# TensorE's loop over the eight experts written out as straight code

## The chip, the cores and the metric

The kernel runs on one NeuronCore of a Trainium2 chip. The metric is device time in microseconds (us) of one execution; lower is better. The kernel before was timed in three runs: median 2112.82 us, lowest 2110.67, highest 2112.97. A separate execution was taken with the hardware profiler; its numbers are those of the profile.

Five engines work side by side, each with its own list of instructions: TensorE (PE in the profile; its weight loads are PEld), VectorE (DVE), ScalarE (ACT), GpSimd (POOL) and SyncE (SP), which here only starts transfers. They meet through semaphores.

## The reference

A sequence of 256 tokens with 1024 features passes through two mixer layers, the second of which ends in a mixture of eight experts, and then through two layers of another block. What the change touches is the mixture of experts:

```python
def moe_swiglu(xn, router_w, w_gate_up, w_down):
    b_, s_, d_ = xn.shape
    xf = xn.reshape(-1, d_)
    logits = (xf @ router_w).astype(jnp.float32)
    top_v, top_i = lax.top_k(logits, TOP_K)
    top_w = jax.nn.softmax(top_v, axis=-1)
    combine = jnp.sum(jax.nn.one_hot(top_i, N_EXPERTS, dtype=jnp.float32) * top_w[..., None],
                      axis=1).astype(xn.dtype)
    out = jnp.zeros_like(xf)
    for e in range(N_EXPERTS):
        out = out + combine[:, e:e + 1] * swiglu(xf, w_gate_up[e], w_down[e])
    return out.reshape(b_, s_, d_)
```

with 8 experts, 2 chosen for each token, and a hidden width of 3584. The weights of one expert are 1024 x 7168 and 3584 x 1024 numbers in float32: 44.04 MB.

## The kernel before

The program is one long list for each engine, in stages: mixer, feed-forward network, mixer, router, experts, and two layers of the second block. Nearly all of it is straight code: the Python that writes it runs over constants. The expert stage is an exception. There each engine has a hardware loop: a body that is in the program once, a register `e` that counts, and a branch from the end of the body back to its start.

For each expert, up to 96 tokens are gathered (`xg`, four groups of 32 columns are used at a time, so one matmul covers a quarter of the array). `token_experts` holds TensorE's part. Its inner function `expert(e, follows)` does, in this order:

- `up("EG", 0, e)` and `up("EU", 0, e)`: gate and up projection of the first 2048 hidden units, four weight tiles of 2 MB each (L1371, 128x512 results);
- the first of the four tiles of `up("EG", 1, e)`, then `first_half_turned`: the hidden values are transposed (L1089), and the numbers of the rows that the next expert needs are computed (L1426);
- the rest of `up("EG", 1, e)` and `up("EU", 1, e)`: the other 1536 hidden units, tiles of 1.5 MB (L1371, 128x384);
- `down(0, e, o)`, the transposes of the second half and, where another expert follows, of the rows gathered for it (L1089), then `down(1..6, e, o)`: the down projection in seven tiles of 2 MB (L1407).

In all an expert has 16 tiles of up weights and 7 of down weights. The function is written into the loop for experts 0 to 6 (`follows` true) and once more behind it for expert 7 (`follows` false). In the profile a float32 matmul of the source appears as two matmuls and two weight loads: 768 of L1371 and 672 of L1407 for each expert.

Waits in the body name a semaphore and a value. In the loop the value is computed from the register `e` (`at(e, ...)`, `tiles.before(name, e)`, `freed(job, i)`); in `begin` a wait whose value is known and not above zero is left out.

The weights come through a ring of five slots of 2 MB. SP's list has its own loop (L955): for every tile it waits until TensorE has freed the slot (`tile_free`, L916) and starts two transfers (L919). So a tile is asked for when the one five places earlier has been used. ScalarE's and VectorE's loops (L2321, L3165) evict results from the banks and form the hidden values; GpSimd's (L1935) fetches the rows of the next expert.

Behind the expert stage the second block begins with the matmuls of L1016 at 1611 us. `more` is the register that TensorE loads before the loop and tests after it, for a further pass that is only run when an expert has more than 96 tokens; the profile shows no such pass.

Of the kernel before, what the change touches and what calls it, by code (L numbers as in the profile page):

```python
# [33 lines left out]
D_FF, EXPERTS, D_EXP = 2816, 8, 3584  # L34
# [365 lines left out]
def kernel_program(nc, t):  # L400
# [30 lines left out]
    with ctx:  # L431
# [354 lines left out]
        def drained(job, i=None):  # L786
            r, s = (banks_f, f_bank_free) if job in banks_f.place else (banks, bank_free)
            return s[r.slot(job)], r.freed(job, i) + 1
# [21 lines left out]
        def at(i, per, n):  # L810
            return n if i is None else i * per + n
# [168 lines left out]
        def _(pe):  # L980
            def begin(job, i=None):

                r, s = (banks_f, f_bank_free) if job in banks_f.place else (banks, bank_free)
                known = i is None or isinstance(i, int)
                if not known or r.freed(job, i) > 0:
                    pe.wait_ge(s[r.slot(job)], r.freed(job, i))
                return bank[r.slot(job)]

            def end(job, i=None):

                if job in closes:
                    return tile_end(closes[job])
                if closing_half(job, i) is not None:
                    return raw_end(closing_half(job, i))
                r, s = (banks_f, f_bank_full) if job in banks_f.place else (banks, bank_full)
                return s[r.slot(job)], 1
# [88 lines left out]
            def turn(job, src, i=None, order=ident):  # L1085

                o = begin(job, i)
                for k, v in enumerate(src):
                    mm = pe.transpose(o[:, k * P:(k + 1) * P], v, order)  # L1089
                mm.then_inc(*end(job, i))  # L1090
# [266 lines left out]
            def token_experts(meanwhile):  # L1357
# [19 lines left out]
                def up(kind, half, e, between=None):  # L1377
                    o = [begin((kind, "m", half, i), e) for i in range(TRIPLE)]
                    for k in range(4):
                        up_tile(kind, half, k, e, o)  # L1380
                        if k == 0 and between is not None:
                            between()

                def turn_gated(half, e):
                    for i in range(TRIPLE):
                        pe.wait_ge(*drained(("EU", "m", half, i), e))
                        turn(("ET", "m", half, i), [gated[half][:, i, k * P:(k + 1) * P] for k in range(UNITS_OF[half] // P)], e)

                def turn_sel(job, groups, e):
                    o = begin(job, e)  # L1390
                    for k, (i, b) in enumerate((i, b) for i in groups for b in range(TB)):
                        for z in range(QUADS):
                            mm = pe.matmul(o[GROUP * z:GROUP * (z + 1), k * P:(k + 1) * P],
                                           sel[:, b, GROUP * i:GROUP * (i + 1)], ident, start=True, stop=True)
                    mm.then_inc(*end(job, e))

                def down(k, e, o):
                    name = ("ED", "m", k)
                    weights(name, e)
                    w = tile_view(name, 4, D)  # L1400
                    for c in range(4):
                        n = 4 * k + c
                        half = n >= HALF // P
                        z, jb = divmod(n - half * HALF // P, UNITS_OF[half] // P)
                        for i in range(TRIPLE):
                            for q in range(QUADS):
                                mm = pe.matmul(o[i // 2][GROUP * q:GROUP * (q + 1), Q_D * (i % 2):Q_D * (i % 2 + 1)],  # L1407
                                               hidT_m[half][:, i, jb, GROUP * z:GROUP * (z + 1)],
                                               w[:, c, Q_D * q:Q_D * (q + 1)], start=n == 0 and i != 1,
                                               stop=n == EX_CH - 1 and i != 0)  # L1410
                            if n == EX_CH - 1 and i == 1:
                                mm.then_inc(*end(("Y", "m", 0)))
                    mm.then_inc(*tile_end(name))

                def expert(e, follows):
                    pe.wait_ge(*drained(("GX", "m", 1), e))
                    up("EG", 0, e)
                    up("EU", 0, e)

                    def first_half_turned():  # L1420
                        turn_gated(0, e)
                        if follows:
                            pe.wait_ge(sel_ready, e + 2)
                            o = begin(("IX", "m"), e)
                            for b in range(TB):
                                mm = pe.matmul(o[:, 0:8], sel_r[:, b, :], token_ids[:, b, :], start=b == 0, stop=b == TB - 1)  # L1426
                            mm.then_inc(*end(("IX", "m")))
                        else:
                            turn_sel(("IX", "m"), (0, 1), e)

                    up("EG", 1, e, first_half_turned)
                    up("EU", 1, e)
                    o = [begin(("Y", "m", n), e) for n in range(2)]
                    for i in range(TRIPLE):
                        pe.wait_ge(*drained(("ET", "m", 0, i), e))
                    down(0, e, o)
                    turn_gated(1, e)
                    if follows:
                        pe.wait_ge(rows_fetched, at(e, 16, 16))
                        for hf in range(2):  # L1440
                            turn(("GX", "m", hf), [x_rows[:, c * P:(c + 1) * P] for c in range(4 * hf, 4 * hf + 4)], e + 1)
                    else:
                        turn_sel(("SX",), (2,), None)
                    for k in range(1, EX_PAIRS):
                        if 4 * (k + 1) > HALF // P >= 4 * k:
                            for i in range(TRIPLE):
                                pe.wait_ge(*drained(("ET", "m", 1, i), e))
                        down(k, e, o)
# [2 lines left out]
                pe.wait_ge(flag_ready, 1)  # L1451
                more = pe.value_load(flag_word)
                meanwhile()
                with pe.Fori(0, EXPERTS - 1) as e:
                    expert(e, True)
                expert(EXPERTS - 1, False)
                return more

            def experts(r, sel_sem):
# [144 lines left out]
            def last_keys():  # L1604
                memory_keys(0, 1, False).then_inc(*end(("EK", 0)))
                memory_keys(1, 1, False).then_inc(*end(("EK", 1)))

            more = token_experts(last_keys)
            pe.br_cond(more > 0, "tensor_overflow", "tensor_second_block")
            home = nc.cur_bb  # L1610
# [2046 lines left out]
```

## Time and profile before

| | |
|---|---|
| median of three runs | 2112.82 us (2110.67 to 2112.97) |
| span of the profiled execution | 2110.0 us |
| TensorE busy | 2067.8 us, 98% of the span |
| VectorE, ScalarE, GpSimd busy | 857.3, 699.9, 46.7 us |
| moved by DMA | 570.95 MB, mean 271 GB/s |
| expert stage, from the first L1371 matmul to the first L1016 matmul behind it | 668.1 to 1611.1 us |

The profiled execution has a span of 2110.0 us; the times of the runs lie 0.7 to 3.0 us above it, the median 2.8 us. Busy time of an engine says how much of the span it was working, not how much could be saved: what counts is the engine that sets the end, and the stretches in which that engine stands still or works slower than it could. The profile also gives the granted clock of TensorE (1.00 is the full 2.4 GHz, 0.50 is 1.2 GHz) for any stretch, and the share in which the core's 16 DMA engines were busy (a little above 1 where packets overlap).

### The profile page before, as it was taken

To read this page: it belongs to the slowest core of one execution; us is meant where nothing else is said; L and a number is where in the kernel's file an instruction comes from. 1 tells how busy PE (TensorE), PEld (TensorE's weight loads), DVE (VectorE), ACT (ScalarE), POOL (GpSimd) and SP (SyncE) were. 2 spreads that over 40 slices of the span, in tenths; PEclk is the share of its full clock that TensorE was granted. 3 is DMA by queue.
4 is the path that set the end of the run, shared out by engine and by line. 5 is a ranking of instruction groups with operands and counts; after the bars stand their busy time and mean duration, and the time that the engine had idled before them with its cause. 6 is when DMAs were issued, how large, how long until landed. Compare 5 with 4: busy or idle time off the path is not lost.

```text
span 2110.0 us, 40789 instructions
## 1 busy us (share of the span) xinstructions
PE 2067.8 (98%) x17747; PEld 1371.6 (65%) x17747; DVE 857.3 (41%) x1203; ACT 699.9 (33%) x950; POOL 46.7 (2%) x69
## 2 busy tenths in 40 slices
PE   9999999999999989989999999999999999999998
PEld 6888888888887343525344353524447888888887
DVE  6876655468764000000000000000024878677775
ACT  5565544455653000001000000001004455555552
POOL 5000000000000000000000000000000000000000
PEclk9999999999999999999999999999999999999999
DMA  9654655554557998999989898999998644455442
GB/s 300 163 183 154 228 190 180 177 197 155 200 180 277 382 413 332 412 355 391 403 346 412 333 413 334 411 358 388 418 394 324 206 146 159 147 195 185 140 160 81
DMA packets 174391, 570.95 MB, mean 271 GB/s; under 512 B 13209, under 2 KB 26273, under 8 KB 157570
## 3 DMA queue, kind: packets, MB, share of 16 engines
q1 hardware_dynamic: 165376, 546.74, 69.9%
q0 software_dynamic: 5280, 17.16, 2.5%
q10 hardware_dynamic: 3554, 4.33, 0.6%
q8 instruction: 151, 2.47, 0.5%
q14 instruction: 30, 0.25, 0.0%
HBM read 562.80 MB, written 5.39 MB: 269 GB/s over the span
## 4 chain that ended last, share of the span: by engine, by line
PE 97%; issue 2%; DMA 1%; DVE 0%; ACT 0%; DVEq 0%; POOL 0%; SPq 0%; ACTq 0%; POOLq 0%
PE bank L1016 39%; PE bank L1371 28%; PE bank L1407 13%; PE bank L1071 5%; PE bank L1089 3%; PE bank L1078 3%; PE bank L1022 1%; DMA ring<-moe_w_down 1%; PE bank L1115 0%; PE bank L1637 0%; PE bank L1644 0%; PE bank L1645 0%; PE bank L1665 0%; PE bank L1651 0%; PE bank L1643 0%
## 5 line engine op out<-in xcount | busy, mean ns | idle before, releaser
L1371 PE MATMUL bank<-ring,xT 128*32 128x512 f32 (+1 forms) x6144 | 591.9, 547 | 31.0 <-issue 31.0
L1016 PE MATMUL bank<-halves_r,x_both 128*128 128x512 f32 x2624 | 607.8, 390 | 0.0
L1016 PEld LDWEIGHTS bank<-halves_r,x_both 128*128 128x128 f32 x2624 | 489.9, 188 | 101.8 <-issue 1.5
L1371 PEld LDWEIGHTS bank<-ring,xT 128*32 128x32 f32 x6144 | 195.7, 111 | 419.6 <-issue 419.2
L2607 DVE TENSOR_TENSOR halves_r<-ring,halves_r 128x2048 fp32r<-128x2048 f32 x170 | 383.8, 2288 | 124.0 <-ACT halves_r L2025 122.9
L2025 ACT ACTIVATE halves_r<-ring 128x2048 fp32r<-128x2048 f32 x172 | 324.9, 1913 | 157.6 <-DMA ring<-w_in 69.7
L3136 DVE TENSOR_TENSOR arena<-arena,bank 128x512 f32<-128x512 f32 (+1 forms) x48 | 29.8, 621 | 773.8 <-PE bank L1371 772.4
L1407 PE MATMUL bank<-ring,arena 128*32 128x256 f32 x5376 | 293.4, 379 | 0.5 <-DMA ring<-moe_w_down 0.5
L1407 PEld LDWEIGHTS bank<-ring,arena 128*32 128x32 f32 x5376 | 175.7, 110 | 115.9 <-issue 5.2
L2288 ACT ACTIVATE arena<-bank 128x512 f32<-128x512 f32 (+1 forms) x48 | 22.6, 545 | 360.3 <-PE bank L1089 360.3
L2212 ACT ACTIVATE arena<-bank 128x512 f32<-128x512 f32 (+1 forms) x58 | 32.1, 554 | 285.0 <-PE bank L1371 252.4
L1071 PE MATMUL bank<-x_both,halves_r 128*128 128x512 f32 x448 | 107.3, 391 | 0.3 <-DVE x_both L3421 0.3
L1071 PEld LDWEIGHTS bank<-x_both,halves_r 128*128 128x128 f32 x448 | 82.4, 188 | 18.4 <-issue 1.6
L1016 PE MATMUL bank<-halves_r,yT_high 128*128 128x512 f32 x256 | 80.7, 392 | 0.0
L2301 ACT ACTIVATE arena<-bank 128x512 f32<-128x512 f32 (+1 forms) x14 | 6.1, 487 | 210.8 <-PE bank L1407 210.8
L1089 PE MATMUL bank<-consts,arena 128*128 128x128 f32 x508 | 65.4, 274 | 0.0
L1089 PEld LDWEIGHTS bank<-consts,arena 128*128 128x128 f32 x508 | 57.1, 141 | 11.1 <-issue 8.3
L1078 PEld LDWEIGHTS bank<-x_both,halves_r 128*128 128x128 f32 x448 | 57.4, 191 | 2.2
L1078 PE MATMUL bank<-x_both,halves_r 128*128 128x256 f32 x448 | 58.1, 283 | 0.0
L1016 PE MATMUL bank<-halves_r,hidT_high 128*128 128x512 f32 x176 | 55.0, 391 | 0.0
L1016 PEld LDWEIGHTS bank<-halves_r,yT_high 128*128 128x128 f32 x256 | 47.9, 188 | 9.8
L2003 ACT ACTIVATE arena<-bank 128x512 f32<-128x512 f32 x54 | 30.9, 597 | 68.0 <-PE bank L1016 54.1
(412 smaller groups left out, 1533.2 us busy)
## 6 DMA issues: line engine op xcount, KB each, us to landing
ring<-moe_w_gate_up SPq DMA_DIRECT2D x128, 1024.0 KB, 13.1
ring<-moe_w_down SPq DMA_DIRECT2D x112, 1024.0 KB, 11.4
ring<-w_in SPq DMA_DIRECT2D x99, 1024.0 KB, 5.2
ring<-moe_w_gate_up SPq DMA_DIRECT2D x128, 768.0 KB, 8.5
ring<-w_out SPq DMA_DIRECT2D x24, 1024.0 KB, 5.0
ring<-ffn_w_gate_up SPq DMA_DIRECT2D x20, 1024.0 KB, 5.3
ring<-ffn_w_down SPq DMA_DIRECT2D x11, 1024.0 KB, 4.9
ring<-w_in SPq DMA_DIRECT2D x18, 512.0 KB, 6.4
```

The lines of the kernel that those rows point to most:

```text
L1016: return pe.matmul(o[:, a:a + n], x[:, c, b * P:(b + 1) * P], w[:, k, col:col + n], **flags)
L1071: mm = pe.matmul(shaped(o[:, :], 2, SEQ), w[:, k, j * P:(j + 1) * P], x_pair[:, :, c, :], start=c == 0, stop=False)
L1078: mm = pe.matmul(o[:, 0:SEQ], w[:, k, j * P:(j + 1) * P], xT_high[:, c, :], start=False, stop=c == KC - 1)
L1089: mm = pe.transpose(o[:, k * P:(k + 1) * P], v, order)
L1371: mm = pe.matmul(o[i][GROUP * z:GROUP * (z + 1), 0:u], xg[:, c, GROUP * i:GROUP * (i + 1)], w[:, q, u * z:u * (z + 1)], start=c == 0, stop ...
L1407: mm = pe.matmul(o[i // 2][GROUP * q:GROUP * (q + 1), Q_D * (i % 2):Q_D * (i % 2 + 1)], hidT_m[half][:, i, jb, GROUP * z:GROUP * (z + 1)], ...
L2003: act.activation(dst, src, func, scale=scale).then_inc(*fr(job))
L2025: act.activation(top_view(half), raw_view(half), ACT.Copy).then_inc(top_in, 1)
L2212: act.activation(dst, out_of(job)[:, 0:n], ACT.Silu).then_inc(*fr(job))
L2288: act.activation(flat(hidT_m[half][:, i, :, :]), out_of(("ET", "m", half, i))[:, 0:UNITS_OF[half]], ACT.Copy).then_inc(*fr(("ET", "m", hal ...
L2607: dve.tensor_tensor(raw_view(half, halves_r), raw_view(half), top_view(half).bitcast(F32), ALU.subtract).then_inc(raw_low_in, 1)
L3136: dve.tensor_tensor(v, v, out_of(("EU", "m", half, i))[:, 0:UNITS_OF[half]], ALU.mult).then_inc(*fr(("EU", "m", half, i)))
```

## The change

In `token_experts`, the loop of TensorE is taken out. A Python loop calls `expert` eight times with a constant `e`, so the body is in TensorE's list eight times, with constant values in its waits. No other engine's list is changed; the loops of SP, ScalarE, VectorE and GpSimd stay.

```diff
--- before.py
+++ after.py
@@ -1451,9 +1451,8 @@
                 pe.wait_ge(flag_ready, 1)
                 more = pe.value_load(flag_word)
                 meanwhile()
-                with pe.Fori(0, EXPERTS - 1) as e:
-                    expert(e, True)
-                expert(EXPERTS - 1, False)
+                for e in range(EXPERTS):
+                    expert(e, e < EXPERTS - 1)
                 return more
```

## Rows read from the trace of the kernel before

**Rows 1.** The page: span; busy time and share; tenths in 40 slices; chain by engine.
```profile
span 2110.0 us, 40789 instructions
PE 2067.8 (98%) x17747; PEld 1371.6 (65%) x17747; DVE 857.3 (41%) x1203; ACT 699.9 (33%) x950; POOL 46.7 (2%) x69
...
PEclk9999999999999999999999999999999999999999
...
PE 97%; issue 2%; DMA 1%; DVE 0%; ACT 0%; DVEq 0%; POOL 0%; SPq 0%; ACTq 0%; POOLq 0%
```

**Rows 2.** TensorE's waits, 640 to 1612 us: releaser, total us, times, longest.
```profile
PE bank L1371 <- issue: 31.0, 6, 5.3
PE bank L1407 <- DMA ring<-moe_w_down: 0.5, 1, 0.5
```

**Rows 3.** TensorE's timeline, expert 0: start, length, instructions [idle before, releaser].
```profile
668.13 45.28 PE L1371 MATMUL bank<-ring,xT 128*32 128x512 f32 x432
...
714.92 27.30 PE L1371 MATMUL bank<-ring,xT 128*32 128x384 f32 x336
...
749.33 31.29 PE L1407 MATMUL bank<-ring,arena 128*32 128x256 f32 x576
```

**Rows 4.** The same timeline: the first block of experts 1 to 7, with expert 1's second.
```profile
785.96 47.25 PE L1371 MATMUL bank<-ring,xT 128*32 128x512 f32 x432 [5.34 <-issue]
...
834.72 27.30 PE L1371 MATMUL bank<-ring,xT 128*32 128x384 f32 x336
...
905.70 47.11 PE L1371 MATMUL bank<-ring,xT 128*32 128x512 f32 x432 [5.28 <-issue]
...
1025.11 47.15 PE L1371 MATMUL bank<-ring,xT 128*32 128x512 f32 x432 [5.08 <-issue]
...
1144.53 47.16 PE L1371 MATMUL bank<-ring,xT 128*32 128x512 f32 x432 [5.07 <-issue]
...
1264.02 47.16 PE L1371 MATMUL bank<-ring,xT 128*32 128x512 f32 x432 [5.11 <-issue]
...
1383.52 47.14 PE L1371 MATMUL bank<-ring,xT 128*32 128x512 f32 x432 [5.13 <-issue]
...
1497.68 45.25 PE L1371 MATMUL bank<-ring,xT 128*32 128x512 f32 x432
```

**Rows 5.** Stretches: us, busy (count) by engine, granted clock, DMA share, GB/s.
```profile
16.00:640.00 624.00, 624.00 (x2982) 516.38 (x2981) 416.34 (x480) 340.55 (x411) 23.58 (x34) 1.00 0.58 187
780.00:786.00 6.00, 0.66 (x16) 0.18 (x11) 0.00 (x0) 2.15 (x3) 0.00 (x0) 0.76 1.01 415
786.00:790.00 4.00, 4.00 (x20) 0.95 (x24) 0.00 (x0) 0.00 (x0) 0.00 (x0) 0.50 1.02 416
790.00:795.00 5.00, 5.00 (x52) 1.47 (x48) 0.00 (x0) 0.00 (x0) 0.00 (x0) 1.00 1.01 404
1612.00:2100.00 488.00, 487.07 (x2697) 419.26 (x2696) 363.77 (x559) 259.37 (x355) 3.72 (x7) 1.00 0.49 162
```

**Rows 6.** The same view, for the transfers: the last two columns, DMA share and GB/s.
```profile
749.00:780.00 31.00, 31.00 (x572) 18.65 (x574) 0.65 (x3) 1.15 (x3) 0.00 (x0) 1.00 1.03 413
786.00:833.00 47.00, 47.00 (x432) 13.45 (x432) 2.07 (x3) 1.79 (x3) 0.00 (x0) 0.96 0.87 332
1430.60:1466.60 36.00, 36.00 (x470) 17.35 (x467) 1.82 (x4) 4.49 (x10) 0.94 (x1) 1.00 1.00 396
1497.70:1518.00 20.30, 20.30 (x196) 6.23 (x192) 0.00 (x0) 1.59 (x4) 0.00 (x0) 1.00 1.02 421
1518.00:1543.00 25.00, 25.00 (x249) 7.80 (x238) 2.06 (x3) 0.87 (x2) 0.00 (x0) 1.00 0.98 384
```

**Rows 7.** DMA queues from 785.9 to 905.6: packets, MB, share of 16 engines.
```profile
q1 hardware_dynamic: 8416, 44.04, 93.1%
q0 software_dynamic: 144, 0.52, 1.2%
q10 hardware_dynamic: 446, 0.39, 1.0%
q8 instruction: 13, 0.21, 0.8%
```

**Rows 8.** The instruction queue, 668.1 to 780.6 and then 1497.7 to 1611.
```profile
q8 instruction: 11, 0.18, 0.6%
...
q8 instruction: 12, 0.20, 0.7%
```

**Rows 9.** SP's loads: expert 1's first tile, its last up tile, expert 7's first tile.
```profile
L919 SPq DMA_DIRECT2D ring<-moe_w_gate_up x2: 356/360/363, 760.2 to 760.7; - x2
DMA to landing us min/median/max: 13.4/14.9/16.5
...
L919 SPq DMA_DIRECT2D ring<-moe_w_gate_up x2: 333/400/467, 842.9 to 843.4; - x2
DMA to landing us min/median/max: 9.4/11.0/12.7
...
L919 SPq DMA_DIRECT2D ring<-moe_w_gate_up x2: 345/345/345, 1477.4 to 1477.9; - x2
DMA to landing us min/median/max: 13.4/14.8/16.1
```

**Rows 10.** SP's waits, 1497 to 1611 us: us, times, longest.
```profile
SPq L916 <- PE bank L1371: 56.7, 14, 9.2
SPq L916 <- PE bank L1407: 13.8, 3, 5.7
```

**Rows 11.** The fetch of the next expert's rows: start of the instruction, time to landing.
```profile
L1940 POOL DMA_INDIRECT arena<-normalised_rows,arena x1: 965/965/965, 836.1 to 836.1; - x1
...
DMA to landing us min/median/max: 9.4/9.4/9.4
```

**Rows 12.** ScalarE's timeline about the end of expert 1.
```profile
900.06 0.87 ACT L2301 ACTIVATE arena<-bank 128x512 f32<-128x512 f32 x2 [30.11 <-PE bank L1407]
...
926.70 0.60 ACT L2212 ACTIVATE arena<-bank 128x512 f32<-128x512 f32 x1 [22.20 <-PE bank L1371]
```

## The prediction

> **What bounds the kernel now.** The page comes first: TensorE is busy for 98% of the span and makes up 97% of the chain that ended last, so the end is set by TensorE, and only its own idle or slow time can be saved. The chain has 2% of "issue" beside it: time in which TensorE waited for nothing that the profile shows [rows 1]. The view of TensorE's waits says where that is: six waits before L1371, 31.0 us together, and in the whole expert stage only one other, of 0.5 us [rows 2]. The timeline then places the six. They stand before the first matmul of experts 1 to 6, each 5.07 to 5.34 us long. There is none before expert 0, where the loop is entered, and none before expert 7, where it is left [rows 3, 4]. The loop over experts 0 to 6 has exactly six branches back. The same body, the same waits on semaphores and the same tiles come at the step from expert 6 to 7, without a gap; only the branch back is missing there. So I read the idle as the price of that branch: TensorE's sequencer has no instructions until the start of the body has been brought in again.
>
> **A second cost at the same place.** The first block of an expert (432 matmuls) takes 45.28 us in expert 0 and 45.25 us in expert 7, but 47.11 to 47.25 us in experts 1 to 6 [rows 3, 4]. The clock explains it: the granted clock falls within the gap (0.76 over 780 to 786), is 0.50, that is 1.2 GHz, over the first 4 us of work after it, and then 1.00; 20 matmuls start in 4 us there, against 52 in the next 5 us [rows 5]. Four us at half speed lose 2 us, which is what the block is longer by.
>
> **What the change removes.** First the gaps: 5.34 + 5.28 + 5.08 + 5.07 + 5.11 + 5.13 = 31.0 us. Then the slow starts: the six blocks sum to 282.97 us, six at the mean of experts 0 and 7 (45.265) would be 271.59, so 11.4 us. Together 42.4 us. The check is by periods. From expert 0's first matmul to expert 7's there are 1497.68 - 668.13 = 829.55 us. Expert 0's period is 785.96 - 668.13 = 117.83 us with one gap and a fast start; without its gap it is 112.49 us. Seven of these are 787.4 us, so 42.1 us go [rows 3, 4]. I take 42.2. All of it is on the path, since TensorE is the path.
>
> **Registers and waits.** In the loop each wait's value is worked out from a register; straight code has constants, and some waits at the start vanish. The bound from the nearest rows: the first block costs 45.28 us in the loop and 45.25 us with constants [rows 3, 4], and both are paced by the matmuls. Taken over three or four blocks of seven experts it is at most 1 us of gain; I take nothing. It can hardly cost anything, as expert 7 is already such code.
>
> **What the change adds.** The body is in TensorE's list eight times in place of two. Its bytes were fetched for every expert before too: the instruction queue brought 0.21 MB in expert 1, against 0.18 MB in expert 0 and 0.20 MB in the straight expert 7 [rows 7, 8]. The traffic stays, and straight code has been fetched in time all through: experts 0 and 7 and the 624 us before 640 have no such wait [rows 2, 5]. Taken at nothing. Were one fetch per expert late, it would cost a gap again.
>
> **What is late next: the weights.** This is the step that could spoil it. During the gap the DMA engines went on filling the ring, and afterwards they had rest: their share over the next block is 0.87 at 332 GB/s [rows 6]. Without gaps the same bytes must come in a shorter period. Per expert they are 44.04 MB of weights, 0.52 of gathered rows, 0.39 of written results and 0.19 of instructions (the mean of the two gapless experts), 45.1 MB [rows 7, 8]; in 119.5 us that is 377 GB/s, in 112.5 us it is 401. What the engines can do is in the stretches where their share is 1: 413 GB/s while down tiles are used, 396 in the second half of the up tiles, 421 at the beginning of expert 7 [rows 6]. Split by stage: (16.78 + 0.39 + 0.05) MB at 417 (between the 413 and the 421) are 41.3 us; (12.58 + 0.52 + 0.07) at 396 are 33.3; 14.75 at 413 are 35.7; in all 110.3 us, 2% below 112.5. That is close, but it fits. The better proof is in the two experts that already start without a gap. In expert 7 the rate falls to 384 GB/s and the share to 0.98 in the second part of the first block [rows 6], since SP was waiting for slots: 17 waits on TensorE, 70.5 us in that expert [rows 10]. Expert 7's first tile was started at 1477.9, landed 16.1 us later at 1494.0 and was used at 1497.68, 3.7 us later [rows 4, 9]. Expert 1's landed at 760.7 + 16.5 = 777.2; expert 0's work ends at 749.33 + 31.29 = 780.6, so 3.4 us are left when the gap is gone [rows 3, 9]. The tightest tile I find is the last up tile of expert 1: landed at 843.4 + 12.7 = 856.1, used six sevenths through the block, at 834.72 + 23.4 = 858.1 [rows 4, 9]. The margins are 2 to 4 us, and a long lead at an expert's start does not reach the end of that expert: by there expert 1, which began with a gap, stands no better than expert 7's first tile did. So I expect no steady stall. Bounds: 0 us if every tile keeps its margin; 0.5 us per expert, 3.5 us, if a wait as in [rows 2] comes once in each; I take 0, since experts 0 to 6 show none.
>
> [...]
>
> **Other engines.** Nothing else was late at the boundary. ScalarE's last eviction of expert 1 starts at 900.06, right behind TensorE's end, and its next work waits 22.20 us for TensorE [rows 12]; after the change it would wait some 15. The rows of the next expert are asked for at 836.1 and land 9.4 us later, at 845.5; TensorE turns them behind the first down tile, past 862 [rows 4, 11]. Both lie within a body and don't move against TensorE.
>
> **Forecast.** Span 2110.0 - 42.2 = 2067.8 us; the median of the runs lies 2.8 us above the profiled span, so 2112.8 - 42.2 = 2070.6 us. Chance 0.76.
>
> **Rivals.**
> - *The DMA engines become the bound (0.15).* For: 401 GB/s wanted, against stretches of 396. Against: the idle share in expert 7. If every stage ran 2.5% below its rows, an expert would take 110.3 x 1.025 = 113.1 us, 0.6 us more than TensorE needs, 4 us over seven; at 4% below, 114.7 us, 2.2 us more, 15 us. That gives 2075 to 2086 us, and waits of L1371 or L1407 on DMA in place of "issue".
> - *It is not the branch (0.04).* If the gap belonged to the start of an expert (a wait that the profile can't name), it would stay: 2112 us. Against: experts 0 and 7 have none. If half stayed, 2092 us.
> - *Slower: TensorE starved of straight code (0.03).* Fetches of instructions queue behind weights that need 13 to 16 us to land [rows 9], in engines now busier. A late fetch costs what the branch does, 5.2 us and 1.9 us of slow clock, 7.1 us. It decides from more than one late fetch per expert: two each are 14 x 7.1 - 42.2, some 57 us over now, 2170 us. Against: the body's 11 to 13 packets per expert [rows 7, 8] came in time in every expert.
> - *The work without rest lowers the clock (0.02).* 624 and 488 us of unbroken work at 1.00 speak against it [rows 5].
>
> **Chances.** A measurement of this kernel can tell about 0.2%, 4 us, from no change. Faster by more: forecast, DMA case and the half case, 0.94. Within: 0.03. Slower: 0.03. The range runs from 2067 (1 us for registers, 2.6 us for the runs' own spread of 2.3 us) to 2080, which takes in the stalls of 3.5 us and the near half of the DMA case; the rest is left out.
>
> **What would show it.** Right: no "issue" wait before L1371; granted clock 1.00 from 668 to the end; first blocks of 45.3 us; periods of 112.5 us for all experts; DMA share near 1 and about 395 to 400 GB/s over the stage; second block's first matmul at about 1569. Wrong: waits on ring<-moe_w_gate_up or moe_w_down that return in each expert (the DMA step failed); "issue" waits inside an expert (the fetch step); a period above 112.5 with no wait (the pace of the matmuls themselves).

## The result and the profile after

The changed kernel takes 2066.5 us (median of 4 runs, 2065.51 to 2067.99) against 2112.89 us for the kernel before (4 runs); the ratio is 0.9782, interval 0.9768 to 0.9796. That is 46.4 us, where 42.2 had been forecast. The time lies 4.1 us under the forecast of 2070.6 us and 0.5 us under the low end of the range.

The page of the changed kernel, the lines that answer to [rows 1]:

```profile
span 2065.6 us, 40648 instructions
...
PEclk9999999999999999999999999999999999999999
...
PE 96%; DMA 2%; DVE 1%; ACT 0%; issue 0%; SPq 0%; DVEq 0%; POOL 0%; ACTq 0%; POOLq 0%
```

The 2% of "issue" in the chain are gone. Of TensorE's waits in the expert stage (660 to 1567 us) one line is left, where [rows 2] had two:

```profile
PE bank L1407 <- DMA ring<-moe_w_down: 1.3, 2, 0.6
```

TensorE's timeline, the first block of experts 0, 1, 2 and 7, which answers to [rows 3, 4] (experts 3 to 6 repeat expert 2's row, 112.28 us apart), then the two waits and the start of the second block:

```profile
666.34 45.28 PE L1371 MATMUL bank<-ring,xT 128*32 128x512 f32 x432
...
778.64 45.25 PE L1371 MATMUL bank<-ring,xT 128*32 128x512 f32 x432
...
890.92 45.25 PE L1371 MATMUL bank<-ring,xT 128*32 128x512 f32 x432
...
1452.33 45.25 PE L1371 MATMUL bank<-ring,xT 128*32 128x512 f32 x432
...
1527.77 5.39 PE L1407 MATMUL bank<-ring,arena 128*32 128x256 f32 x96 [0.62 <-DMA ring<-moe_w_down]
...
1551.04 15.75 PE L1407 MATMUL bank<-ring,arena 128*32 128x256 f32 x288 [0.64 <-DMA ring<-moe_w_down]
1566.72 0.50 PE L1016 MATMUL bank<-halves_r,mg_high_a 128*128 128x512 f32 x1
```

No row has a wait at an expert's start, and each first block takes 45.3 us. The stretches of the changed kernel, in the columns of [rows 5] (the last three: granted clock, DMA share, GB/s): experts 0 to 6 as a whole, then both parts of expert 1's first block:

```profile
666.30:1452.30 786.00, 786.00 (x10298) 350.16 (x10301) 31.11 (x67) 65.53 (x120) 6.67 (x7) 1.00 1.00 401
778.60:799.00 20.40, 20.40 (x198) 6.24 (x192) 0.00 (x0) 2.98 (x5) 0.00 (x0) 1.00 1.01 420
799.00:823.80 24.80, 24.80 (x244) 7.67 (x236) 2.07 (x3) 0.83 (x2) 0.00 (x0) 1.00 0.98 385
```

TensorE never rests in 786 us, its clock is 1.00 throughout, and the transfers run at 401 GB/s with a share of 1.00. Over the same experts the kernel before had:

```profile
668.10:1497.70 829.60, 798.59 (x10301) 346.77 (x10304) 31.11 (x67) 65.58 (x120) 6.67 (x7) 0.98 0.96 380
```

**Where the time went, by spans.** The span fell by 44.4 us. From expert 0's first matmul to expert 7's: 829.55 us before, 1452.33 - 666.34 = 785.99 after, 43.56 less. Expert 7: 1611.08 - 1497.68 = 113.40 before, 114.39 after, 0.99 more. Ahead of the stage: it starts at 666.34 in place of 668.13, 1.79 less. Behind it: 498.92 and 498.88, nothing. 43.56 - 0.99 + 1.79 + 0.04 = 44.4.

### The profile page after: what moved, and what is told of

The parts are those of the page before. It is cut to its first block, busy times and chain, and to the rows that moved or that the text cites. A ratio compares the mean times of both kernels' runs of the same rounds, so it can differ in the third digit from the quotient of the medians.

```text
span 2065.6 us, 40648 instructions
## 1 busy us (share of the span) xinstructions
PE 2053.3 (99%) x17747; PEld 1373.8 (67%) x17747; DVE 857.0 (41%) x1203; ACT 699.7 (34%) x950; POOL 46.7 (2%) x69
## 4 chain that ended last, share of the span: by engine, by line
PE 96%; DMA 2%; DVE 1%; ACT 0%; issue 0%; SPq 0%; DVEq 0%; POOL 0%; ACTq 0%; POOLq 0%
PE bank L1016 39%; PE bank L1371 27%; PE bank L1407 13%; PE bank L1071 5%; PE bank L1089 3%; PE bank L1078 2%; DMA ring<-moe_w_down 2%; PE bank L1022 1%; DMA ring<-w_in 1%; PE bank L1115 0%; PE bank L1636 0%; PE bank L1644 0%; PE bank L1643 0%; PE bank L1664 0%; PE bank L1650 0%; PE bank L1642 0%
## 5 line engine op out<-in xcount | busy, mean ns | idle before, releaser
L1016 PE MATMUL bank<-halves_r,x_both 128*128 128x512 f32 x2624 | 607.8, 390 | 0.0
L1371 PE MATMUL bank<-ring,xT 128*32 128x512 f32 (+1 forms) x6144 | 580.4, 539 | 0.0
L1016 PEld LDWEIGHTS bank<-halves_r,x_both 128*128 128x128 f32 x2624 | 489.9, 188 | 101.9 <-issue 1.5
L1371 PEld LDWEIGHTS bank<-ring,xT 128*32 128x32 f32 x6144 | 198.8, 110 | 372.9 <-issue 371.4
L1407 PE MATMUL bank<-ring,arena 128*32 128x256 f32 x5376 | 293.4, 379 | 1.3 <-DMA ring<-moe_w_down 1.3
L1407 PEld LDWEIGHTS bank<-ring,arena 128*32 128x32 f32 x5376 | 176.4, 110 | 116.1 <-issue 6.3
L1016 PE MATMUL bank<-halves_r,yT_high 128*128 128x512 f32 x256 | 80.7, 392 | 0.0
L1016 PE MATMUL bank<-halves_r,hidT_high 128*128 128x512 f32 x176 | 55.0, 391 | 0.0
L1016 PEld LDWEIGHTS bank<-halves_r,yT_high 128*128 128x128 f32 x256 | 47.9, 188 | 9.8
```

The source lines that it names most:

```text
L1016: return pe.matmul(o[:, a:a + n], x[:, c, b * P:(b + 1) * P], w[:, k, col:col + n], **flags)
L1371: mm = pe.matmul(o[i][GROUP * z:GROUP * (z + 1), 0:u], xg[:, c, GROUP * i:GROUP * (i + 1)], w[:, q, u * z:u * (z + 1)], start=c == 0, stop ...
```

## The experiments

Each ran beside the kernel before, on the same chip as it. Two theories stood at first: the gap is the fetch of code at the branch's target, or it is the loop's own cost (registers, compares).

### e1: the changed kernel again

> The changed kernel as it is, in five rounds. Open: of the 46 us between the medians the traces explain 44.4 (43.6 at the boundaries, 1.8 from an earlier full clock at the start, 1.0 lost in expert 7). If the boundaries are all of it, and the start is chance, the median of the pairs lies 42.5 to 43.6 us under the kernel before (ratio 0.9794 to 0.9799) and the periods are again 112.28 us. If straight code also brings something outside of the expert stage, the difference stays at 45 to 46 us (ratio 0.9782 or less), and TensorE's first L1371 matmul comes earlier than 668.1 us in every profile of the straight kernel.

Measured: 2066.64 us (5 runs) against 2111.69 (9 runs), ratio 0.9785, interval 0.9772 to 0.9799: 45.0 us. From expert 0's first matmul to expert 7's again 785.98 us, but the stage began at 664.44 us. The ratio lies between the two cases that were expected and decides for neither. The start of the stage is dealt with under e9 and e10.

### e2: the loop kept, its branch announced

```diff
-                with pe.Fori(0, EXPERTS - 1) as e:
+                with nc.Fori(0, EXPERTS - 1, engines=bass.OrderedEngineSet([pe.engine]), hint_back_edge=True) as e:
                     expert(e, True)
```

```profile
778.39 45.25 PE L1371 MATMUL bank<-ring,xT 128*32 128x512 f32 x432
...
890.67 45.25 PE L1371 MATMUL bank<-ring,xT 128*32 128x512 f32 x432
...
1452.07 2.74 PE L1371 MATMUL bank<-ring,xT 128*32 128x512 f32 x19
1457.13 45.25 PE L1371 MATMUL bank<-ring,xT 128*32 128x512 f32 x413 [2.32 <-issue]
...
1455.00:1461.00 6.00, 3.87 (x21) 0.98 (x25) 0.00 (x0) 0.00 (x0) 0.00 (x0) 0.72 1.01 416
```

The loop is there, with its registers, compares and six branches back, and all six gaps are gone, with the slow starts behind them. The two kernels have the same work and the same six branches; what is new is that their target is named ahead. So the theory of the code fetch holds against the loop's own cost. The DMA queue of instructions agrees with it. Here, at the first boundary, one of its packets starts at 774.40 us and the next at 780.92, and TensorE works on without a stop past 778.39: the head of the body was there ahead of the branch. In the kernel before the packets start at 776.77 and 782.94, and TensorE stands still from 780.62 to 785.96. Expert 1 takes 12 packets here and 13 there:

```profile
q8 instruction: 12, 0.20, 0.7%
```

A new gap of 2.32 us stands 19 matmuls behind the last pass. There the announced branch is not taken and the code behind the loop is wanted, which is my reading of it; an instruction packet starts at 1454.78 us, as the gap opens at 1454.81, and ends 1.3 us before the gap does. The granted clock is 0.72 over the 6 us from 1455 on. The 413 matmuls behind the gap take as long as 432 elsewhere, 2.0 us too long, and 2.3 + 2.0 are the 4.3 us that remain against the straight kernel.

### e3: straight code with loops of one pass

```diff
-                for e in range(EXPERTS):
-                    expert(e, e < EXPERTS - 1)
+                for k in range(EXPERTS - 1):
+                    with pe.Fori(k, k + 1) as e:
+                        expert(e, True)
+                expert(EXPERTS - 1, False)
```

> Straight code for experts 0 to 6, but each inside a loop of its own of one pass: the count is a register, every wait's value is worked out from it and the compare at the end is there, but no branch back is taken. Theory: no gap over 0.5 us at the boundaries, periods of 112.3 us, time within 2 us of the straight kernel. Rival (registers and compares cost time): 1 us or more per expert, 7 us or more over the straight kernel.

Measured: 2067.38 us (4 runs), ratio 0.9786, interval 0.9771 to 0.9801. First blocks of experts 1 and 2:

```profile
780.55 45.25 PE L1371 MATMUL bank<-ring,xT 128*32 128x512 f32 x432
...
892.83 45.25 PE L1371 MATMUL bank<-ring,xT 128*32 128x512 f32 x432
```

There is no issue wait in the stage, and the periods are 112.28 us, as without any loop. Registers and compares cost nothing that can be seen: the second theory falls, and the term taken at nothing in the sum was right.

### e4: two experts in a pass

```diff
-                with pe.Fori(0, EXPERTS - 1) as e:
+                with pe.Fori(0, EXPERTS - 2, 2) as e:
                     expert(e, True)
+                    expert(e + 1, True)
+                expert(EXPERTS - 2, True)
                 expert(EXPERTS - 1, False)
```

> Loop of three passes with two experts each (0 to 5), then experts 6 and 7 straight: two branches back in place of six. Theory: two gaps of 5.1 to 5.3 us, before experts 2 and 4, each with a first block of 47.1 us behind it; 2 x 7.2 = 14.4 us over the straight kernel, 2081 us. Rival (the gap grows with the size of the body that is jumped over): the two gaps are longer, up to 10 us each, 2090 us.

Measured: 2082.16 us (4 runs), ratio 0.9860, interval 0.9845 to 0.9875; 2081 was expected.

```profile
896.51 46.74 PE L1371 MATMUL bank<-ring,xT 128*32 128x512 f32 x432 [5.11 <-issue]
...
1127.84 47.12 PE L1371 MATMUL bank<-ring,xT 128*32 128x512 f32 x432 [5.10 <-issue]
```

Two branches, two gaps, as long as with half the body: 15.5 us over the straight kernel of e1, 7.8 for each branch (7.2 expected). By the timelines, from expert 0 to expert 7, it is 799.92 against 785.98 us, 7.0 for each. Between one expert and two in the body, the price goes by the number of branches and not by the body's length.

### e5: bodies of five sizes, transfers at rest

```diff
+                    for size in (1, 5, 10, 20, 32):
+                        with pe.Fori(0, 3):
+                            for _ in range(size):
...
+                                            pe.matmul(o[i][GROUP * z:GROUP * (z + 1), 0:WIDE], xg[:, q, GROUP * i:GROUP * (i + 1)],
+                                                      w[:, q, WIDE * z:WIDE * (z + 1)], start=True, stop=True)
```

> The straight kernel with added work ahead of expert 0's first real matmul: five loops of three passes each, whose bodies are 96, 480, 960, 1920 and 3072 matmuls and weight loads of L1371's kind on the first tile (their results are overwritten). The transfers are at rest in that time, the ring being full. It measures the branch back by itself. Theory (code that is no longer held must be fetched): short bodies show no gap above 0.5 us, the largest shows two gaps, and the small step lies somewhere between; a gap may be shorter than 5.1 us, about 2 to 4 us, as no weights compete. Rival (each branch back costs the same): ten gaps of about 5 us. Rival (the price grows with the body): gaps in proportion to the body's length.

Measured in one run, TensorE's timeline. The bodies hold 48, 240, 480, 960 and 1536 matmuls, and as many weight loads; three passes of the first three and one of the fourth are the 3264 of the first row:

```profile
666.05 350.41 PE L1387 MATMUL bank<-ring,xT 128*32 128x512 f32 x3264
1017.54 103.21 PE L1387 MATMUL bank<-ring,xT 128*32 128x512 f32 x960 [1.09 <-issue]
1121.47 268.01 PE L1387 MATMUL bank<-ring,xT 128*32 128x512 f32 x2496 [0.72 <-issue]
1390.28 165.01 PE L1387 MATMUL bank<-ring,xT 128*32 128x512 f32 x1536 [0.80 <-issue]
1556.20 165.01 PE L1387 MATMUL bank<-ring,xT 128*32 128x512 f32 x1536 [0.91 <-issue]
```

Six branches back over bodies of up to 960 matmuls and weight loads cost nothing. Four over 1920 and 3072 cost 0.7 to 1.1 us each. With the transfers at rest there is a size up to which a loop is free, between 960 and 1920.

The instruction queue shows what is different between them. Its packets, first pass and then both further passes of the third body (758.8 to 810.4, 810.4 to 913.4 us), then pass by pass of the fourth (from 913.4, 1017.5 and 1121.4) and of the fifth (from 1224.6, 1390.2 and 1556.2):

```profile
q8 instruction: 4, 0.07, 0.5%
...
DMA packets 0, 0.00 MB, mean 0 GB/s; under 512 B 0, under 2 KB 0, under 8 KB 0
...
q8 instruction: 8, 0.13, 0.5%
...
q8 instruction: 9, 0.15, 0.6%
...
q8 instruction: 8, 0.13, 0.5%
...
q8 instruction: 13, 0.21, 0.6%
...
q8 instruction: 14, 0.23, 0.6%
...
q8 instruction: 13, 0.21, 0.5%
```

A body of 960 matmuls and weight loads is brought once and run three times; one of 1920 or 3072 is brought again in every pass. So code that is no longer held is fetched, and here the branch cost time only where it was.

But the price here is under the 2 to 4 us expected, and a fifth or less of the kernel's 5.1 to 5.4 us. Two things differ: the transfers rest, and the matmuls ahead of the branch are 512 columns wide where the kernel's (L1407) are 256. e11 and e12 take one each.

### e11: the loop with few transfers at the branch

```diff
+                thin = name[0] in ("EG", "EU") and name[2] == 0 and not isinstance(i, int)
                 for a, b, src in pieces:
+                    if thin:
+                        sp.dma_start(v[:, a:b, 0:WIDE], src[:, :, 0:WIDE]).then_inc(fu[r.slot(name)], 16)
+                        continue
```

> The kernel before with its loop, but for experts 1 to 7 the eight up tiles of the first 2048 hidden units load only a quarter of their columns (the rest of a slot keeps old weights, which leaves part of the projection out). So the DMA engines are mostly at rest while TensorE ends an expert and branches back, and the branch is the same. Theory (the fetch of code queues behind weights): the six gaps shrink from 5.2 us to about 1 us, as in the loops of e5, the clock stays at 1.00, about 2070 us. Rival (the gap is long because down matmuls are short and leave little queued work to cover the fetch, whatever the transfers do): the gaps stay at 4 to 5 us, about 2105 to 2112 us.

Measured in one run: 2090.42 us. The first two of the six gaps, and the stretch about the first (DMA share 0.38):

```profile
780.94 46.97 PE L1375 MATMUL bank<-ring,xT 128*32 128x512 f32 x432 [2.49 <-issue]
898.04 46.68 PE L1375 MATMUL bank<-ring,xT 128*32 128x512 f32 x432 [2.92 <-issue]
...
775.00:781.00 6.00, 3.51 (x68) 1.89 (x64) 0.00 (x0) 0.87 (x2) 0.00 (x0) 1.00 0.38 124
```

The gaps are 2.49 to 2.96 us (16.7 in all), at a DMA share of 0.4 to 0.5 within them: neither the 1 us of the theory nor the 4 to 5 us of the rival. About half of the price goes with the load on the DMA engines. The last instruction packet ahead of TensorE's restart starts 0.3 to 0.4 us before the last matmul ends; in the kernel before it starts 2.1 to 2.4 us after that end. It takes 0.9 to 1.5 us here and 1.0 to 1.1 there. So what the weights' transfers cost the fetch is a start about 2.5 us later, not a slower packet. The slow clock was expected to go and did not: four of six first blocks take 46.7 to 47.0 us. The other two, behind gaps of 2.55 and 2.96 us, take 45.28, so the gap's length alone does not decide it.

### e12: bodies of one size, results of three widths, transfers at rest

```diff
-                    for size in (1, 5, 10, 20, 32):
+                    for size, width in ((1, 256), (32, WIDE), (32, 256), (32, 128)):
```

> As e5, transfers at rest, but with large bodies alone (3072 matmuls and weight loads) whose results are 512, 256 and 128 columns wide, three passes each, behind a short loop of 96. Open is why the branch costs 0.7 to 1.1 us in e5 and still 2.5 to 3.0 us in e11, where the transfers are at 0.4. Theory (matmuls already handed to the engine go on running while code is fetched, so the gap is the fetch less the length of what is queued): 0.8 to 1.0 us with 512 columns as in e5, about 2 to 3 us with 256 columns (half as long each), 3 to 4 us with 128. Rival (only the transfers decide): 0.7 to 1.1 us at all widths.

The matmuls write `width` columns. Measured in one run. The rows ahead of which the six branches stand, two for each width:

```profile
842.13 165.01 PE L1387 MATMUL bank<-ring,xT 128*32 128x512 f32 x1536 [1.28 <-issue]
1008.20 247.89 PE L1387 MATMUL bank<-ring,xT 128*32 128x512 f32 x3072 [1.05 <-issue]
1258.38 83.46 PE L1387 MATMUL bank<-ring,xT 128*32 128x256 f32 x1536 [2.30 <-issue]
1343.77 3.22 PE L1387 MATMUL bank<-ring,xT 128*32 128x256 f32 x52 [1.93 <-issue]
...
1473.93 43.87 PE L1387 MATMUL bank<-ring,xT 128*32 128x128 f32 x1458 [3.29 <-issue]
...
1523.73 32.05 PE L1387 MATMUL bank<-ring,xT 128*32 128x128 f32 x1074 [3.25 <-issue]
```

1.2 us with 512 columns, 2.1 with 256, 3.3 with 128 (means of two): the faster the matmuls ahead of the branch, the longer TensorE stands still. Five more waits of 0.3 us each lie inside the bodies of narrower matmuls. TensorE works on while code is fetched: the last instruction packet ahead of the restart starts 1.2 and 1.6 us before the last matmul's end with 512 columns, 0.4 and 0.6 us before it with 256, and 0.6 and 0.9 us after it with 128. By the means of two that is 2.1 us more work left beside the fetch with 512 columns than with 128, and the gaps differ by 2.1 us. With the kernel's own width the price is 2.1 us with transfers at rest, 2.5 to 3.0 at a share of 0.4 to 0.5 (e11), and 5.1 to 5.4 at 1.01 [rows 4, 5]. So both things that differed, the width and the transfers, raise the price, and at the kernel's values of both it is the kernel's gap.

### e6, e7, e8: how much room the transfers have

```diff
+                pool.dma_start(spare_dram.ap(), t["moe_w_down"][0, 0, 0:256, :]).then_inc(extra_in, 16)
+                pool.wait_ge(extra_in, e * 16 + 16)
```

(behind the fetch of the next expert's rows, in GpSimd's loop; 768 rows in e7 and e8).

> The straight kernel; in each of GpSimd's seven passes a copy of 1.05 MB from HBM to HBM is added behind the fetch of the next expert's rows. It tests how much room the transfers have. By my sum an expert needs 110.3 of 112.3 us of transfer time, and the copy takes 2.5 us at 413 GB/s: 0 to 0.6 us per expert, 2066 to 2071 us. Rival (much more room than the sum says): no change, and no wait on DMA. Rival (a burst of 2.5 us beats the lead of 2 to 4 us of a tile, whatever the mean): 1 to 2 us per expert, 2073 to 2081 us, in waits on the tiles right behind the copy.

Measured: 2078.68 us (4 runs), ratio 0.9837, interval 0.9818 to 0.9855: 12.1 us over the straight kernel, 1.7 for each copy, where the sum gave 0 to 0.6. The rival of the burst held. TensorE's waits:

```profile
PE bank L1409 <- DMA ring<-moe_w_down: 8.3, 8, 1.6
...
PE bank L1373 <- DMA ring<-moe_w_gate_up: 1.8, 3, 1.0
```

> The same with 3.15 MB per expert, 7.6 us of transfer time at 413 GB/s. By the sum 7.6 - 2.0 = 5.6 us more per expert, 39 us in seven, 2106 us, with waits of L1371 and L1407 on the ring. Rival (much room): under 1 us per expert, below 2074 us.

Measured: 2127.59 us (4 runs), ratio 1.0075, interval 1.0053 to 1.0098: 61 us over the straight kernel, where 39 were expected.

> The kernel before with the same 3.15 MB per expert. Its period of 119.5 us has 9.2 us of room by the sum, more than the copy's 7.6 us: no change, 2112 to 2116 us, so that the straight code's gain shrinks from 46 to some 8 us. Rival (the copy's cost does not depend on the period): as much slower as the straight kernel becomes.

Measured: 2179.43 us (4 runs), ratio 1.0326, interval 1.0308 to 1.0343: 69 us over the kernel before, where nothing was expected. The rival held: the copy costs the loop no less than the straight code, and the straight code stays 52 us ahead. Expert 1 of e8, and the stretch behind its wait:

```profile
841.09 15.69 PE L1373 MATMUL bank<-ring,xT 128*32 128x384 f32 x192
864.24 13.67 PE L1373 MATMUL bank<-ring,xT 128*32 128x384 f32 x144 [7.47 <-DMA ring<-moe_w_gate_up]
...
866.00:880.00 14.00, 14.00 (x180) 5.48 (x176) 1.67 (x3) 0.00 (x0) 0.00 (x0) 0.93 1.02 412
```

and all of TensorE's waits in its expert stage:

```profile
PE bank L1373 <- DMA ring<-moe_w_gate_up: 46.7, 7, 7.5
PE bank L1373 <- issue: 31.3, 6, 5.3
```

Each copy makes one wait of 5.7 to 7.5 us, which ends some 20 us after the copy is started, on top of the six issue gaps. Behind the wait the granted clock falls as it does behind a gap: 0.73 over 857 to 866 us and 0.93 over 866 to 880. The room of the loop's period was of no use to it: it lies in the first block (share 0.87 [rows 6]), and the copy falls into the second half, where the share is 1 in either kernel and a tile lands 2 to 4 us ahead of its use. A sum over a period says whether the mean fits; it does not say what a burst costs.

### e9 and e10: both kernels again on one chip

> The kernel before against itself, for a second profile of it. If the first profile's late start of the expert stage (668.1 us, full clock from 15 us on) was chance, the stage now starts at 664 to 668 us, while the stage itself repeats: 829.5 us from expert 0's first matmul to expert 7's, six gaps of 5.1 to 5.3 us. If the straight code also changed something ahead of the stage, it starts at 668 us again. The runs should spread over some 4 us, as those beside the other kernels did.

> The changed kernel once more, on the same chip as the second profile of the kernel before. From first to last expert 786.0 us; expert 7 with 0.9 to 1.3 us of waits on DMA; median 2066 to 2067 us. The stages give 42.6 us of difference; if the runs' medians differ by 44 us or more again, more than the expert stage has changed or the start favours one of the two.

Measured: the kernel before 2111.14 us (11 runs), against itself 0.9995, interval 0.9986 to 1.0004; the straight kernel 2066.60 us, ratio 0.9783, interval 0.9770 to 0.9797. The kernel before as the partner in these pairs: median 2112.38 us, 2107.15 to 2115.14 in 15 runs; the straight kernel's five lie between 2065.27 and 2067.50. Spans of the two profiles: 2109.0 and 2065.7. Three rows of e9, experts 0, 1 and 4:

```profile
666.60 45.28 PE L1371 MATMUL bank<-ring,xT 128*32 128x512 f32 x432
784.18 47.49 PE L1371 MATMUL bank<-ring,xT 128*32 128x512 f32 x432 [5.08 <-issue]
...
1143.61 46.97 PE L1371 MATMUL bank<-ring,xT 128*32 128x512 f32 x432 [5.36 <-issue]
```

Expert 0 to 7: 829.72 us in e9, 785.99 in e10. The stage starts at 666.60 and 666.38 us. In the twelve other profiles, whose code ahead of the stage is the same, it starts between 664.4 and 668.2 us: straight ones at 666.34, 664.44 and 668.24 (after, e1, e3), with the loop at 668.13, 666.09 and 666.63 (before, e2, e4). The start does not go with the kernel. The expectations put it down to the clock, which the rows do not show: in eight profiles (before, after, e1 to e4, e9, e10) the granted clock reads 1.00 over the first 16 us. What differs is the pace and the waits there: the first two 128x512 matmuls of L1153 take 2.07 us before, and 1.12 or 1.13 us in the other seven. Why, stays open.

## Why the prediction was right and wrong

The mechanism held. What failed is the size: the step from the profiled span to the median, and the start of the stage, which the sum took as fixed.

**What bounds, and the branch: right.** What TensorE lost at the boundaries came off the span in full: 31.0 us of gaps, 11.4 us of slow starts and 1.1 us that the sum had missed (below) are the 43.56 us. That six branches back are six gaps was shown by e2 (same loop, branches announced, no gaps), e4 (two branches, two gaps) and e3 (no branch back taken, no gap). That the price is a wait for code is inferred from e2, and from e5, where branches over short bodies are free. The instruction queue shows the fetch itself. For the last of its packets ahead of the restart (from the DMA view in narrow windows, where a packet is counted at its start and its share gives its length):

| run | gaps | their length, us | packet starts, from the last matmul's end | packet takes | from its end to the next matmul |
|---|---|---|---|---|---|
| before | 6 | 5.07 to 5.34 | 2.1 to 2.4 after | 1.0 to 1.1 | 1.8 to 2.0 |
| e4 | 2 | 5.11, 5.10 | 2.1 after | 1.1, 1.0 | 1.9, 2.0 |
| e11 | 6 | 2.49 to 2.96 | 0.3 to 0.4 before | 0.9 to 1.5 | 1.8 to 2.0 |
| e5 | 4 | 0.72 to 1.09 | 1.6 to 1.7 before | 0.9 to 1.2 | 1.4 to 1.6 |
| e12 | 6 | 1.05 to 3.29 | 1.6 before to 0.9 after | 0.9 to 1.3 | 1.4 to 1.6 |

In all 24 gaps TensorE goes on 1.4 to 2.0 us after such a packet has landed, whatever the gap's length, where in straight work the queue brings one in 6 to 15 us. That agrees with the prediction's reading, that TensorE has nothing to run until the start of the body has been brought in again. It also bears on the third rival. Fetches do come later beside weights (before against e11), and a late one cost 7.0 us with its slow clock (e4), near the 7.1 taken; but in straight code none was late.

**The slow starts: right.** 11.4 us were read from the blocks of 47.1 to 47.3 us; all blocks are now 45.25 or 45.28 us, at a clock of 1.00. The pace follows the granted clock: in the kernel before, groups of four weight loads of L1371 start 0.85 us apart at 0.50 and 0.43 us apart at 1.00. The 2.4 GHz of the full clock are an estimate here, one column taken as one cycle: at 1.00 the 128x512 matmuls of L1016 start 226.6 ns apart (30 in 6.96 us, the last 0.39 us long) and the 128x256 ones of L1022 120 ns apart, so 256 columns more take 106.6 ns, 2.4 columns per ns.

**The period of 112.49 us: too long by 0.2 us.** The measured one is 112.28. I took expert 0's period less its idle time. But idle time is counted from the modelled end of the last matmul, and in work without a gap the next matmul starts before that end. It stood in the rows: expert 0's down block is 31.29 us long [rows 3], while in the timeline of the changed kernel the step from 747.54 to 778.64 is 31.10. A gap thus costs 0.19 us more than the idle time shown, 1.1 us for six, and 42.4 and 1.1 make 43.5. 43.56 us went in place of the 42.2 taken, 1.4 of the 4.1 that were missed.

**The anchor: the step that failed.** The forecast was a span of 2067.8 us plus 2.8 us, "the median of the runs lies 2.8 us above the profiled span". For the changed kernel this term measured 2066.5 - 2065.6 = 0.9 us, so 1.9 us of the miss lie in it. One and the same execution is 1.8 us longer than its span: 2067.41 with 2065.6, and 2110.76 with 2109.0 in e9. The rest of the 2.8 was the spread of the runs: one profiled execution and three timed runs were small samples of runs that lie between 2107.2 and 2115.2 us in all the pairs here, and I carried their difference over as if it were fixed.

**The span itself: 2.2 us too long.** That is 1.4 us for the period (above) and 1.8 us because the stage started earlier in the second profile, less the 1.0 us that expert 7 lost; the sum had the last two at nothing. 2.2 + 1.9 = 4.1. The low end of the range was set too near: it allowed 3.6 us below the forecast, while the start of the stage alone moves by 3.8. The first profile began the stage at 668.13 us, near the late end of the 664.4 to 668.2 of all profiles; that part of the miss is bad luck.

Taken over the profiles alone, the stage as a whole is 942.95 and 943.46 us (before, e9) against 900.38, 900.26 and 900.41 (after, e1, e10): 42.9 us. The runs say more: 44.5 to 46.4 us by medians in each pairing, and over all 47 runs of the kernel before (median 2111.7) and 14 of the changed one (median 2066.6) 45.1 us; resampled, the means of these runs differ by 44.5 to 45.9 us, which leaves 42.9 out. Where these 2 us lie, no trace shows: the stage may be longer in runs that were not profiled, or something outside of it may differ. It stays open.

**The weights: right in the outcome.** No wait in experts 0 to 6, 401 GB/s as worked out, a share of 0.98 in the second part of the first block. Expert 1's first tile lands at 758.9 + 16.5 = 775.4 and is used at 778.64, 3.2 us later; 3.4 were forecast:

```profile
L919 SPq DMA_DIRECT2D ring<-moe_w_gate_up x2: 355/360/364, 758.4 to 758.9; - x2
DMA to landing us min/median/max: 13.6/15.0/16.5
```

But the "2% below" was not room that could be used, and the idle share in expert 7, on which the prediction leaned, did not show such room either: 1.05 MB more per expert, 2.5 us of transfer, cost 1.7 us (e6). The rival of the DMA bound is nearer than its chance of 0.15 looks. Its first signs are the waits in expert 7, 0.5 us before and 0.9 to 1.3 us in the straight kernel's profiles; e9 had 0.8 with the loop, so part of them is chance.

**Code supply, other engines: right.** Instructions came in time in all eight straight experts; no issue wait is left. The instruction queue brought 80 packets over experts 0 to 6, against 89 with the loop. ScalarE's wait at the boundary went from 22.20 us [rows 12] to 14.86, 15 expected.

## What to carry to other kernels

An idle stretch of the bounding engine that the profile gives as "issue", once per pass and not at the loop's entry or exit, points at the branch back (here six of 5.07 to 5.34 us): count the branches, take the idle time and the slower work behind it, and take the period from a step without a gap, not from the idle time. Write the body out, or announce the branch where code must stay small (e2: all six gaps gone, 4.3 us over the straight kernel); a loop whose body is short was free here, up to 960 matmuls and weight loads with the transfers at rest (e5). And when a saving is carried from a profile to a median, use the profiled execution's own time, or leave the difference in the range.

## What the runs showed that had not been expected

- The price of the same branch goes from 0.7 to 5.4 us: 1.2, 2.1 and 3.3 us behind matmuls 512, 256 and 128 columns wide with transfers at rest (e12), 2.5 to 3.0 us at a DMA share of 0.4 to 0.5 (e11), 5.0 to 5.4 us at 1.0, all with large bodies.
- An announced branch costs a gap where it is not taken: 2.32 us once, behind the loop (e2).
- A copy of 3.15 MB from HBM to HBM beside a full stream of weights cost TensorE 5.7 to 7.5 us of waiting and, by the fall of the clock, a slower block after it (144 matmuls in 13.67 us in e8, where 192 ahead of the wait take 15.69), 8.7 us per expert in all in e7.
- Gaps of 2.3 to 3.0 us were enough for a fall of the granted clock in e2 and in four of six cases of e11. In e12 gaps of 3.3 us brought it (0.50 over 1473 to 1478 us) and those of 1.9 and 2.3 us did not. Gaps of 0.7 to 1.1 us in e5 brought none: its clock is 1.00 about the first of them.

```profile
1010.00:1025.00 15.00, 13.91 (x135) 4.06 (x128) 0.00 (x0) 0.00 (x0) 0.00 (x0) 1.00 0.01 2
```
